# Differential attention scores: two 128-row passes per softmax in place of three 64-row passes and a mask

## The reference

```python
s = jnp.einsum('bqhtd,bkhtd->bhtqk', qi, k, preferred_element_type=f32) * scale
mask = key_chunk[None, :] <= q_chunk[:, None]      # chunks of 64 tokens
s = jnp.where(mask, s, -jnp.inf)
p = jax.nn.softmax(s, axis=-1)
pd = p[:, :, 0] - lam * p[:, :, 1]
return jnp.einsum('bhqk,bkhv->bqhv', pd, v)
```

## Time and profile before

| | us |
|---|---|
| median of 3 runs | 3461.07 |
| lowest, highest | 3458.13, 3461.18 |
| span of the profiled execution | 3460.9 |
| TensorE busy in it | 3361.4 (97%) |
| VectorE busy | 2208.2 (64%) |
| ScalarE busy | 1435.1 (41%) |
| GpSimd busy | 1121.9 (32%) |
| differential attention, first score matmul to the last value product | 1788.6 to 2532.8 |
| one head of the loop, first score matmul to the next head's | 94.8 |

### The profile page before, as it was taken

How to read it: one execution, slowest core, us unless ns; L and a number is a source line. 1 busy time by engine, 2 the same in 40 slices (tenths; PEclk the granted TensorE clock), 3 DMA queues, 4 the chain that set the end, 5 groups by cost and what they waited for, 6 DMA issues and landing times.

```text
span 3460.9 us, 44771 instructions
## 1 busy us (share of the span) xinstructions
PE 3361.4 (97%) x16616; PEld 2710.6 (78%) x16616; DVE 2208.2 (64%) x2246; ACT 1435.1 (41%) x1901; POOL 1121.9 (32%) x644
## 2 busy tenths in 40 slices
PE   8899899999999999999999999999889999999998
PEld 6677777888888868888877777777668878888886
DVE  8896968777773474322277888888856574444434
ACT  5688835444441142333223443344453353333213
POOL 2000028888832212111111111111112276766222
PEclk9999999999999999999999999999999999999999
DMA  4210221222252112111111111111122212123322
GB/s 143 62 44 19 73 88 66 84 85 79 85 196 95 47 43 92 36 42 36 36 49 43 37 42 35 38 42 36 43 79 85 79 61 91 74 90 121 134 88 83
DMA packets 59167, 242.52 MB, mean 70 GB/s; under 512 B 6592, under 2 KB 6592, under 8 KB 53312
## 3 DMA queue, kind: packets, MB, share of 16 engines
q1 hardware_dynamic: 59072, 241.22, 19.7%
HBM read 194.53 MB, written 41.42 MB: 68 GB/s over the span
## 4 chain that ended last, share of the span: by engine, by line
PE 81%; DVE 12%; issue 3%; ACT 3%; DMA 0%; POOL 0%; DVEq 0%; POOLq 0%; ACTq 0%
PE ps L506 45%; PE ps L1457 24%; PE ps L2696 2%; PE ps L2708 2%; PE ps L2685 1%; PE ps L2846 1%; PE ps L2859 1%; DVE conv_acc L2310 1%; PE ps L529 1%; DVE t_wide L1094 1%; PE ps L2798 1%; PE ps L2853 1%; PE ps L2832 1%; DVE small L2350 1%; PE ps L2794 1%
## 5 line engine op out<-in xcount | busy, mean ns | idle before, releaser
L477 POOL TENSOR_TENSOR w_lo_part<-w_raw,w_hi_part 128x1024 fp32r<-128x1024 f32 x162 | 404.5, 2497 | 1739.0 <-ACT w_hi_part L460 1739.0
L506 PE MATMUL ps<-h_hi_part,w_hi_part 128*128 128x512 f32 x1904 | 625.4, 409 | 34.9 <-POOL w_lo_part L477 12.4
L506 PE MATMUL ps<-h_lo_part,w_hi_part 128*128 128x512 f32 x1904 | 596.5, 394 | 0.0
L506 PE MATMUL ps<-h_hi_part,w_lo_part 128*128 128x512 f32 x1904 | 594.9, 393 | 0.0
L460 ACT ACTIVATE w_hi_part<-w_raw 128x1024 fp32r<-128x1024 f32 x180 | 189.1, 1051 | 720.0 <-PE ps L506 632.4
L506 PEld LDWEIGHTS ps<-h_hi_part,w_hi_part 128*128 128x128 f32 x1904 | 348.1, 191 | 130.4 <-issue 37.2
L506 PEld LDWEIGHTS ps<-h_lo_part,w_hi_part 128*128 128x128 f32 x1904 | 361.7, 190 | 78.5 <-issue 0.3
L506 PEld LDWEIGHTS ps<-h_hi_part,w_lo_part 128*128 128x128 f32 x1904 | 361.4, 190 | 78.7
L2310 DVE SCALAR_TENSOR_TENSOR conv_acc<-u_pad,cols,conv_acc 128x1024 f32<-128x1024 f32 x232 | 307.4, 1325 | 19.4 <-DVE conv_acc L2310 2.8
L2149 DVE TENSOR_TENSOR residual<-residual,ps 128x1024 f32<-128x1024 f32 (+1 forms) x60 | 73.2, 1221 | 268.7 <-PE ps L506 262.2
L506 PE MATMUL ps<-u_hi,w_hi_part 128*128 128x512 f32 x736 | 232.0, 390 | 0.0
(11 more groups left out here) (446 smaller groups left out, 6583.1 us busy)
## 6 DMA issues: line engine op xcount, KB each, us to landing
w_raw<-in_w SPq DMA_DIRECT2D x226, 512.0 KB, 3.3
w_raw_odd<-in_w SPq DMA_DIRECT2D x46, 512.0 KB, 3.9
u_spill<-ffn_u SPq DMA_DIRECT2D x46, 512.0 KB, 3.0
u_wide<-u_spill SPq DMA_DIRECT2D x23, 1024.0 KB, 9.2
residual<-in_x SPq DMA_DIRECT2D x4, 1024.0 KB, 9.0
both_halves<-q_chan SPq DMA_DIRECT2D x16, 256.0 KB, 4.3
x_again<-in_x SPq DMA_DIRECT2D x8, 512.0 KB, 3.9
residual<-in_x SPq DMA_DIRECT2D x2, 2048.0 KB, 7.2
```

The costliest lines, as they stand in the source:

```text
L477: pool.tensor_tensor(WLO[:, slot], WRAW[:, slot], f32(WHI[:, slot]), ALU.subtract).then_inc(w_ready, 1)
L506: last = pe.matmul(PS[:, ps, b * HALF:(b + 1) * HALF], st[:, slot, k, :], at(mv, k, b), start=(k == 0 and n == 0), stop=(k == nk - 1 and n ...
```

## The change

Each softmax t gets four tiles of its own, all 128 partitions high. "Own" are its 64 partitions, "other" the 64 of the other softmax:

- Q1: high query (own), low query (other). K1: high key in both halves. One 128-row pass of Q1 by K1 gives high by high plus low by high.
- Q2: high query (own), mask rows (other). K2: low key (own), mask rows (other). One pass of Q2 by K2 gives high by low plus the mask. The mask rows are the 8 blocks of queries in 8 rows, and -1e30 for the last 64 keys of a block; DVE writes them once, ahead of the first head (4 instructions where there were 2 small ones).

So a softmax's scores are two passes of full height instead of three of half height and a mask matmul. The number of keys of block 2 is 384 (512 before), of block 6 896 (1024 before).

ACT and DVE prepare more of it: ACT 2 high-query copies of 64x1024 instead of one of 128x1024, 2 high-key copies of 64x1024 instead of one, and 8 copies of 64x512 instead of 4, spread over the head. DVE makes low query and low key in 2 instructions of 64x1024 each instead of 3.

Tiles move to make room; a scratch tile for a Newton step changes; in head 7 the tanh of one output gate (`m_conv_act` 2) moves behind the last exponentials, and the eight gates are computed in another order. The core of the diff:

```diff
+        Q1 = [scratch(f"dq_hi_lo{t}", [P, S], F32R, 2 + t) for t in range(2)]
+        Q2 = [scratch(f"dq_hi_mask{t}", [P, S], F32R, 4 + t) for t in range(2)]
+        K1 = [scratch(f"dk_hi_twice{t}", [P, S], F32R, 6 + t) for t in range(2)]
+        K2 = [scratch(f"dk_lo_mask{t}", [P, S], F32R, (13, 18)[t]) for t in range(2)]
+        OWN, OTHER = (slice(0, HD), slice(HD, P)), (slice(HD, P), slice(0, HD))
...
-            act.activation(DQH[:, :], psl(0), ACT.Copy, scale=HD ** -0.5).then_inc(dq_hi, 1)
-            act.wait_ge(dq_hi, heads * 6 + 1)
             for t in range(2):
-                act.activation(DQHS[64 - 64 * t:128 - 64 * t, :], f32(DQH[64 * t:64 * t + 64, HALF:]), ACT.Copy
-                               ).then_inc(dq_hi, 1)
+                act.activation(Q1[t][OWN[t], :], PS[OWN[t], 0, :], ACT.Copy, scale=HD ** -0.5).then_inc(dq_hi, 1)
             split_act(act, jp + 3, 0)
+            act.wait_ge(dq_hi, heads * 12 + 2)
+            diff_copies_act(act, Q2, Q1, OWN, OWN, LEFT)
+
+        def diff_copies_act(act, to, src, rows_to, rows, cols):
+
+            for t in range(2):
+                act.activation(to[t][rows_to[t], cols], f32(src[t][rows[t], cols]), ACT.Copy).then_inc(dq_hi, 1)
...
             act.wait_ge(job_done, 2 * jp)
-            act.activation(DKH[:, :], psl(1), ACT.Copy).then_inc(dq_hi, 1)
-            act.wait_ge(dq_hi, h * 6 + 4)
             for t in range(2):
-                act.activation(DKHS[64 - 64 * t:128 - 64 * t, :], f32(DKH[64 * t:64 * t + 64, HALF:]), ACT.Copy
-                               ).then_inc(dq_hi, 1)
+                act.activation(K1[t][OWN[t], :], PS[OWN[t], 1, :], ACT.Copy).then_inc(dq_hi, 1)
+            act.wait_ge(dq_hi, h * 12 + 6)
+            diff_copies_act(act, K1, K1, OTHER, OWN, LEFT)
             split_act(act, jp, 1)
...
             evac(0)
+            diff_copies_act(act, K1, K1, OTHER, OWN, RIGHT)
             exp(1, 0)
             exp(1, 1)
             evac(1)
             if jobs:
                 cg()
+            diff_copies_act(act, Q2, Q1, OWN, OWN, RIGHT)
             for qt in (2, 3):
...
+            for t in range(2):
+                dve.wait_ge(dq_hi, h * 12 + (t + 1))
+                ins = dve.scalar_tensor_tensor(Q1[t][OTHER[t], :], PS[OWN[t], 0, :], HD ** -0.5, f32(Q1[t][OWN[t], :]),
+                                               ALU.mult, ALU.subtract)
+            ins.then_inc(ps_free[0], 1)
...
+            for t in range(2):
+                dve.wait_ge(dq_hi, h * 12 + (5 + t))
+                ins = dve.tensor_tensor(K2[t][OWN[t], :], PS[OWN[t], 1, :], f32(K1[t][OWN[t], :]), ALU.subtract)
+            ins.then_inc(ps_free[1], 1)
...
             def scores2(qt):
 
-                n = -(-(qt + 1) * P // 256) * 256
-                for i, (q, k) in enumerate(((DQH, DKH), (DQH, DKL), (DQL, DKH))):
-                    for t in range(2):
-                        rows = slice(64 * t, 64 * t + 64)
-                        pe.matmul(PS[:, 2, HALF * t:HALF * t + n], q[rows, qt * P:qt * P + P], k[rows, 0:n],
-                                  start=(i == 0), stop=False)
+                n, q = max((qt + 1) * P, 256), slice(qt * P, qt * P + P)
                 for t in range(2):
-                    mask(qt, HALF * t + qt * P, slice(64 * t, 64 * t + 64)).then_inc(ds_done, 1)
+                    to = PS[:, 2, HALF * t:HALF * t + n]
+                    pe.matmul(to, Q1[t][:, q], K1[t][:, 0:n], start=True, stop=False)
+                    pe.matmul(to, Q2[t][:, q], K2[t][:, 0:n], start=False, stop=True).then_inc(ds_done, 1)
...
+                n, q = max((qt + 1) * P, HALF + 256), slice(qt * P, qt * P + P)
...
+                for i, (st, mv) in enumerate(((Q1, K1), (Q2, K2))):
+                    pe.matmul(PS[:, 2, 0:HALF], st[t][:, q], mv[t][:, 0:HALF], start=(i == 0), stop=(i == 1))
+                    mm = pe.matmul(PS[:, 2, HALF:n], st[t][:, q], mv[t][:, HALF:n], start=(i == 0), stop=(i == 1))
+                mm.then_inc(ds_done, 1)
```

More of the change, by code:

```diff
@@ L356, in two_blocks @@
         DTM = scratch("dm_tanh", [P, S], F32, 12)
-        DVF = scratch("dv_chan", [P, S], F32, 13)
+        DVF = scratch("dv_chan", [P, S], F32, 14)
         CG = scratch("cg_tanh", [P, S], F32, 14)
-        DO, DSQ, DV, DY = (scratch(f"do_{c}", [P, S], F32, 15 + i) for i, c in enumerate(("out", "sq", "v", "y")))
+        DO, DSQ, DV = (scratch(f"do_{c}", [P, S], F32, 15 + i) for i, c in enumerate(("out", "sq", "v")))
+        DY = scratch("do_y", [P, S], F32, 16)
+        DN = [scratch(f"do_newton{i}", [P, S], F32, t) for i, t in enumerate((14, 19, 18))]
         UC = scratch("u_pad", [P, S + 32], F32, 19)
@@ L1841, in diff_head_act @@
                 evac(qt)
-            if not jobs:
-                m_conv_act(act, 2)
             exp(7, 0)
@@ L1847, in diff_head_act @@
                 diff_q_act(act, jp, h * 16 + 16, h + 1)
+            else:
+                m_conv_act(act, 2)
             evac(7)
@@ L2382, in diff_head_dve @@
             if not first:
-                diff_norm_dve(dve, st, h - 1)
+                diff_norm_dve(dve, st, h - 1, DN[0 if jobs else 1])
             row_max(5, 0)
@@ L2566, in vector_program @@
             dve.wait_ge(gy_done, 8 + PRIMED)
-            st.do(dve.tensor_copy(MQ[:, :], con("mask_q")))
-            st.do(dve.tensor_copy(MK[:, :], CON[:, CONST["mask_k"] + CH:CONST["mask_k"] + P]))
+            for t in range(2):
+                rows, block = OTHER[t], OTHER[t].start + CONST["ident"]
+                for to, pattern in ((Q2, "mask_q"), (K2, "mask_k")):
+                    st.do(dve.tensor_tensor(to[t][rows, :].rearrange("p (b c) -> p b c", c=P),
+                                            CON[rows, block:block + QT].unsqueeze(2).broadcast_to([HD, QT, P]),
+                                            con(pattern)[rows, :].unsqueeze(1).broadcast_to([HD, QT, P]), ALU.mult))
             st.do(dve.memset(UC[:, 0:30], 0.0))
@@ L2820, in fill @@
                         job(pe, jp + n // 2, n % 2, ks=ks)
-            def mask(qt, to, rows):
-                return pe.matmul(PS[:, 2, to + CH:to + P], MQ[rows, :], MK[rows, :], start=False, stop=True)
             def scores2(qt):
-                n = -(-(qt + 1) * P // 256) * 256
-                for i, (q, k) in enumerate(((DQH, DKH), (DQH, DKL), (DQL, DKH))):
-                    for t in range(2):
-                        rows = slice(64 * t, 64 * t + 64)
-                        pe.matmul(PS[:, 2, HALF * t:HALF * t + n], q[rows, qt * P:qt * P + P], k[rows, 0:n],
-                                  start=(i == 0), stop=False)
+                n, q = max((qt + 1) * P, 256), slice(qt * P, qt * P + P)
@@ L2840, in scores @@
                 if t:
                     pe.wait_ge(de_done, h * 16 + (2 * qt + 1))
-                own, other = slice(64 * t, 64 * t + 64), slice(64 - 64 * t, 128 - 64 * t)
-                q0, q1 = slice(qt * P, qt * P + P), slice(qt * P - HALF, qt * P - HALF + P)
-                for i, (q, qs, k, ks) in enumerate(((DQH, DQHS, DKH, DKHS[other, 0:n]), (DQH, DQHS, DKL, DKL[other, HALF:HALF + n]),
-                                                    (DQL, DQLS, DKH, DKHS[other, 0:n]))):
-                    pe.matmul(PS[:, 2, 0:HALF], q[own, q0], k[own, 0:HALF], start=(i == 0), stop=(i == 2))
-                    pe.matmul(PS[:, 2, HALF:HALF + n], qs[other, q1], ks, start=(i == 0), stop=False)
```

46 lines of the change are left out of this document (13 added, 33 removed).

## The result

The changed kernel takes 3470.85 us (median of 5 runs, 3469.93 to 3474.61) against 3461.07 before: ratio 1.0032, 95% interval 1.0022 to 1.0043. It is slower by 9.8 us. The profiled execution's span is 3470.7 us, 9.8 over that of before, so the comparison of the two traces has the whole difference in it.

A forecast was written before the change was run, and what follows sets the result against it. Two nearly equal loops were taken as the bound: TensorE's own (97% busy) and one through ScalarE and VectorE. From 3460.9: +3.6 (heads 1 to 6), -0.4 (head 0), -1.4 (head 7), +3 (clock), forecast 3465.5 us, range 3455 to 3474.

The forecast's parts named there:

- rival B: Every head's block 5 wait halves the clock, a fall in six or more heads: 3471 to 3474 us; chance 0.25.
- C: TensorE gains little: short full-height matmuls take 0.228, or the 0.2 around a block stays; 3469 us; chance 0.1.
- TensorE's part: Score blocks of the differential attention: two full-height passes save TensorE 3.5 us a head, 28 us in 8 heads.
- The query's copies behind the tanh: ScalarE's right-half query copies ahead of block 2's exponentials: not hidden, 1.3 us go whole into VectorE's start on block 2.
- Rival A: TensorE decides and the gain is real, needing half-height copies at under half of 1.3: 3453 us; chance 0.15.
- The second key copy ahead of the squares: Head's start: values and squares come 0.9 later, so TensorE waits some 0.5 us there.
- The loop: Chain through ScalarE and VectorE, cut at block 2's combine: a head goes from 94.79 to 95.4 us, +0.6.
- VectorE's key and query pairs: Low key and low query, two instructions each: 2.36 per pair, from 2.10 and 2.65 before; level.
- the ends 95.1 and 96.2: Head length if all, or none, of VectorE's 1.1 us of waits for TensorE in blocks 3 to 7 go.
- Head 7: Chain of score, maximum, exponential: six score groups of blocks 5 to 7 give about 0.25 each, -1.4 us.
- Head 0: No normalisation on VectorE: TensorE keeps 1.3 of its 3.5, less 0.9 for the late value copy: -0.4 us.
- The clock: Block 5's wait grows to 1.8: three falls in eight heads at 1.0 each, +3 us.

The follow-up runs named there:

- e6: Kernel before with four convolution taps of blocks 0 to 4 narrowed to 64 columns, for timing only: 3450.97 us, ratio 0.9971.
- e7: Changed kernel with the query copies behind block 2 and the same four taps narrowed to 64 columns, for timing only: 3449.84 us.
- e1: Changed kernel with ScalarE's two query right-half copies moved behind block 2's copy out of PSUM: 3463.57 us, ratio to before 1.0008.
- e8: Kernel before with two 64x512 ScalarE query copies added behind the gate's tanh, ahead of block 2's exponentials: 3467.02 us, ratio 1.0019.
- e2: Changed kernel with head 7's moved weight split issued ahead of block 7's exponentials again, the tanh staying behind them: 3468.37 us.
- e5: As e4, but each head's first weight split stands behind block 0's copy out of PSUM: 3452.72 us, ratio to before 0.9977.
- e9: e5 plus, in heads 1 to 6, one filler unit moved ahead of block 5's second softmax scores: 3448.93 us, ratio to before 0.9969.
- e3: Changed kernel with the head's first weight split moved behind the value copy and squares, ahead of block 0's exponentials: 3473.16 us.
- e11: Kernel before with the first split behind block 0's copy out of PSUM and block 5's filler unit moved: 3456.81 us, ratio 0.9990.
- e4: Changed kernel with the three moves of e1, e2 and e3 together: 3458.16 us, ratio to before 0.9997.

## Why the prediction came out as it did

The time, 3470.85, lies in the range (3455 to 3474), but 5.4 over the forecast: slower by 0.3%, where I held no change for likeliest. That the range held is in part luck: its upper end was drawn for rival B, and a term that I had left out, in head 7, came to lie in that room. By the total alone B (3471 to 3474) and C (3469) are nearer than my forecast; what rules them out is the trace. Step by step:

- **TensorE's part: right, and somewhat less than forecast.** Groups of 0.69 and the 256-key matmul at 0.12, as taken. Of the 3.5 a head forecast, 2.8 to 3.0 are found between e6 and e7. In the changed kernel itself the busy time shows 2.2 (93.46 to 91.26), because it stops seven times a head where it stopped twice, and by the starts of the matmuls around it each stop takes some 0.16 beside the wait listed for it: with that, 2.9. Rival C is out: three half-height passes with mask and borders cost more than two full ones. The Trainium skill's rule on row tiling (TensorEngine Tiling (Array Packing), Performance Considerations), which I had put beside C, doesn't decide here.
- **The query's copies behind the tanh: right,** place and size (2.42 for 0.84; e1 and e8 show it both ways). Rival A is out by the same.
- **The second key copy ahead of the squares: right,** 0.68 for some 0.5. The two key copies start 1.04 apart, where I took 0.90.
- **The loop: the right mechanism, a term too small.** To block 2's combine 17.15 (16.9 forecast). Behind it 78.85, so 0.45 less than before, where I took 78.2, with all of VectorE's 1.1 us of waiting gone. Of these 1.1 only 0.6 went: the four waits of 0.26, 0.21, 0.46 and 0.17 ahead of a row maximum became 0.12 each, which is also what VectorE idles there behind a tap when the scores are long ready. VectorE's key and query pairs took 2.46, not 2.36, the key's thus 0.36 more than before. I had the ends 95.1 and 96.2 and chose 95.4; 96.0 is near the other. That is 0.6 in six heads, 3.6 of the 5.4.
- **Head 7: wrong.** -1.4 forecast, +1.8 measured. I had read the move of `m_conv_act` 2 as a move of a tanh. The split in it carries a GpSimd instruction, and of that I priced nothing: 2.0 by e2. That is 3.2 missed in one head, nearly as much as in the six of the loop together. With the copies and the first split moved as well the head takes 78.3 (e5, e9) for 80.4, so the gain on the scores was there.
- **Head 0: right in sign.** It is 2.0 shorter where I took 1.3, and its wait for the values grew by 1.2 where I took 0.9: -0.8 for -0.4.
- **The clock: the effect about right, count and price not.** I forecast three falls at 1.0. Two came in the loop, and clean and disturbed heads differ by 1.3 to 1.4, so of the 1.7 that a fall costs TensorE 0.3 to 0.4 is absorbed, not 0.7. There is one more at head 7's start, but the kernel before has two in its head 7, so that one isn't new. Two at 1.35 make 2.7 for the 3 forecast, which is luck. Rival B, a fall in every head, didn't come about here, but the four falls of e1 and e5 show how near it was.

## What to carry to other kernels

When an engine that is 97% busy gets lighter, price first what the change puts on the others at the one place where the chain through them has no slack: two copies of 0.65 us there made every head 1.2 longer although TensorE had about 3 us less to do in it. Moved by one block they cost nothing, but the head was then only back at its old 94.8: the chain through ScalarE and VectorE has to get shorter too before TensorE's gain is seen. When a step is moved, follow every engine that it starts, and look whom each meets: the split's two-operand instruction on GpSimd stops VectorE's two-operand ones for its whole length. And where an edit shows no gain, look at whether it carries a cost of its own before giving up the reason for it: e3 gained nothing, the same idea with the split 4 us further on gained 1.0 a head (94.8 in e1, 93.8 in e5).

## What the runs showed of the hardware

- A VectorE instruction with two SBUF inputs that begins beside a running GpSimd `tensor_tensor` ends at a fixed distance behind it, however long they overlap: the 128x1 one 0.01 us behind (1.55 for 0.16), a 128x1024 one 1.08 behind (3.26 for 1.29). Both kernels have this twice in every head of the loop as well: at the last tap (2.48, before 2.36) and at a tap near the head's end (1.57, before 1.80), where their neighbours take 1.28. All of these end 1.08 to 1.09 behind GpSimd's instruction. GpSimd's own takes 2.93 instead of 2.4 where it begins inside a running tap. The last tap of the changed kernel:

```profile
2109.53 2.93 POOL L475 TENSOR_TENSOR w_lo_part<-w_raw,w_hi_part 128x1024 fp32r<-128x1024 f32 x1 [18.79 <-ACT w_hi_part L458]
...
2111.07 2.48 DVE L2315 SCALAR_TENSOR_TENSOR conv_acc<-u_pad,cols,conv_acc 128x1024 f32<-128x1024 f32 x1
```

- Nearly the same wait of TensorE, 1.8 to 2.1 us in block 5, is followed by a fall of the granted clock to the 1.2 GHz level in two of six heads of the changed kernel and in four of e1 and e5, and not in the rest. After waits of up to 1.66 there (the kernel before and e6 to e11) none was seen. After the 2.10 to 2.11 of head 1 there was one in four of six kernels and none in e4 and e5. So the length of the wait alone doesn't tell. A fall costs 1.3 to 1.4 us here.
- ScalarE and VectorE take as long for 64 partitions as for 128: VectorE's two 64x1024 subtractions for the key take 2.46 together, one of 128x1024 takes 1.22; ScalarE's two copies of the key from PSUM at 64x1024 take 2.05 together, a copy of 128x1024 takes 1.02.
